# A hybrid decoder block on one core: the third part of w_ada summed on VectorE, its gates made later, and expert loads whose order turns over three experts

## What is computed

```
mod = silu(c) @ w_ada + b_ada          # 6 x 1024: shift, scale, gate for mixer and MoE
h = RMSNorm(x) * (1 + scale1) + shift1
proj = h @ w_in                        # conv B, C, u | q, k, v | gate_a, gate_b
y_a = (B * dwconv3(C * u)) @ w_out_conv ; y_b = diff_attention(q, k, v) @ w_o_attn
x = x + gate1 * ((sigmoid(ga) * y_a + sigmoid(gb) * y_b) @ w_merge)
h = RMSNorm(x) * (1 + scale2) + shift2
x = x + gate2 * MoE(h)                 # top 4 of 32 experts, clamped SwiGLU
out = RMSNorm(x)
```

## Time and profile before

| | us |
|---|---|
| median of 3 runs | 1215.8 |
| lowest, highest run | 1212.63, 1217.0 |
| the profiled execution | 1212.78 |
| its span, first to last instruction | 1211.0 |
| PE busy | 1148.4 (95%) |
| DVE busy | 409.5 (34%) |
| ACT busy | 208.7 (17%) |

### The profile page before, as it was taken

The page is one execution under the profiler, slowest core; times in us unless marked ns, Lnnn a source line. Parts: engine busy times, 40 slices in busy tenths (PEclk is TensorE's granted clock), DMA queues, the critical chain, the costliest instruction groups (busy, mean ns, idle before and its releaser), DMA issues.

```text
span 1211.0 us, 15215 instructions
## 1 busy us (share of the span) xinstructions
PE 1148.4 (95%) x6027; PEld 534.1 (44%) x6027; DVE 409.5 (34%) x795; ACT 208.7 (17%) x333; POOL 19.7 (2%) x40
## 2 busy tenths in 40 slices
PE   5999999999999999999999998989999999999997
PEld 4787899985333333333333332323333333333332
DVE  4447746663232222222222222222232222222222
ACT  4346543341011010101010101010110101010001
POOL 1000010000000000000000000000000000000000
PEclk9999999999999999999999999999999999999999
DMA  9997565798999999999999999999999999999994
GB/s 338 395 386 280 182 230 167 255 398 369 397 428 430 427 430 426 431 426 429 428 429 428 429 428 429 427 382 421 426 432 425 431 426 431 426 430 427 430 426 206
DMA packets 59394, 470.55 MB, mean 389 GB/s; under 512 B 5871, under 2 KB 11196, under 8 KB 32742
## 3 DMA queue, kind: packets, MB, share of 16 engines
q1 hardware_dynamic: 56644, 467.99, 93.5%
q10 hardware_dynamic: 2722, 2.16, 0.6%
HBM read 469.08 MB, written 1.06 MB: 388 GB/s over the span
## 4 chain that ended last, share of the span: by engine, by line
PE 65%; DMA 29%; DVE 2%; ACT 1%; SPq 1%; issue 1%; DVEq 0%; POOLq 0%; POOL 0%; ACTq 0%
PE ps L1014 19%; DMA expert<-in_w_down 16%; PE ps L783 15%; PE ps L1052 15%; DMA expert<-in_w_gate_up 12%; PE ps L988 4%; PE ps L959 2%; PE ps L727 1%; PE ps L658 1%; PE ps L940 1%; PE ps L1039 1%; ACT r_work L1254 1%; SPq L440 1%; DVE r_v L1691 1%; DMA ada_first<-in_w_ada 1%
## 5 line engine op out<-in xcount | busy, mean ns | idle before, releaser
L1014 PE MATMUL ps<-expert,r_work 128*64 128x512 f32 x2048 | 451.7, 594 | 12.3 <-DMA expert<-in_w_gate_up 11.3
L1014 PEld LDWEIGHTS ps<-expert,r_work 128*64 128x64 f32 x2048 | 146.5, 137 | 300.1 <-issue 280.1
L1052 PE MATMUL ps<-expert,r_work 128*64 128x512 f32 x1024 | 233.4, 606 | 24.1 <-DMA expert<-in_w_down 15.9
L1682 DVE TENSOR_SCALAR r_v<-ps 128x512 f32<-128x512 f32 x32 | 22.1, 692 | 371.3 <-PE ps L1014 371.3
L1052 PEld LDWEIGHTS ps<-expert,r_work 128*64 128x64 f32 x1024 | 72.8, 139 | 162.7 <-issue 136.9
L1250 ACT ACTIVATE r_v<-r_v 128x512 f32<-128x512 f32 x32 | 20.2, 630 | 713.8 <-DVE r_v L1682 713.8
L1702 DVE TENSOR_TENSOR r_work<-ps,r_gb 64x512 f32<-64x512 f32 x64 | 44.1, 689 | 169.5 <-PE ps L1052 169.0
L1364 DVE TENSOR_TENSOR w_lo<-stage,w_hi 128x2048 fp32r<-128x2048 f32 x36 | 82.2, 2289 | 55.9 <-ACT w_hi L1110 55.9
L783 PE MATMUL ps<-x_hi,w_hi 128*128 128x256 f32 x304 | 87.6, 288 | 0.0
L783 PE MATMUL ps<-x_lo,w_hi 128*128 128x256 f32 x304 | 86.0, 283 | 0.0
L783 PE MATMUL ps<-x_hi,w_lo 128*128 128x256 f32 x304 | 86.0, 283 | 0.0
(11 more groups left out here) (219 smaller groups left out, 862.3 us busy)
## 6 DMA issues: line engine op xcount, KB each, us to landing
expert<-in_w_gate_up SPq DMA_DIRECT2D x128, 2048.0 KB, 26.9
expert<-in_w_down SPq DMA_DIRECT2D x64, 2048.0 KB, 20.4
stage<-in_w_in SPq DMA_DIRECT2D x24, 1024.0 KB, 5.6
stage<-in_w_ada SPq DMA_DIRECT2D x16, 1024.0 KB, 7.7
ada_first<-in_w_ada SPq DMA_DIRECT2D x16, 256.0 KB, 6.4
ada_first<-in_w_ada SPq DMA_DIRECT2D x8, 512.0 KB, 12.2
stage<-in_w_o_attn SPq DMA_DIRECT2D x4, 1024.0 KB, 7.7
stage<-in_w_merge SPq DMA_DIRECT2D x4, 1024.0 KB, 5.8
```

The costliest lines, as they stand in the source:

```text
L1014: mm = pe.matmul(ps[CAP * g:CAP * g + CAP, j, :], xg[:, 2 * (k % 4) + k // 4, :], buf[:, col:col + 512], start=False, stop=(k == KD - 1))
L1052: mm = pe.matmul(ps[CAP * half:CAP * half + CAP, 3, :], aT[:, ch, CAP * g:CAP * g + CAP], expert[n][:, col:col + 512], start=(q == 0), sto ...
L1682: v.tensor_scalar(glu.rearrange("p (b n) -> p b n", b=2), gu[:, :, :, 0], LIMIT, None, ALU.min).then_inc(glu_ready, 1)
```

## The change

Three edits that belong together, and one of the expert loads.

- Part three of w_ada no longer goes to PE chunk by chunk. DVE scales each 128 x 2048 chunk with silu(c) per partition and adds it up in one tile, ada_acc (`ada_add`, semaphore `ada_added`). When all eight are in, PE adds the partitions with a matrix of ones: four matmuls, `ada_sum`, at the start of step 22. SP now waits for `ada_added` before it reuses a buffer that held such a chunk.
- STREAM is in another order. Part three's first four chunks are loaded behind chunks 3 to 6, part two behind 7 to 14, part three's last four behind 19 to 22. DVE adds a chunk in the step before the one it is loaded with, behind its w_lo of that step: steps 2 to 5 and 18 to 21.
- mod_step moves from steps 19, 20, 21, 22 to 20, 23, 24, 25, the late loads to 22, router weights to 24, router bias to 26. b_parts lies in the place of the keys, and ACT waits there for the scores rather than for the gates. The load of slot 2 waits for the gates too. The subtraction for lambda moves one step on.
- The order of the expert loads turns over experts 16 to 19: in front of `rest_of_next` come four, three, two and one of the slots of the expert after next.

```diff
+ADA_AT = {7 + k: ("ada", 1, k) for k in range(KD)}
+ADA_AT.update({3 + k if k < 4 else 15 + k: ("ada", 2, k) for k in range(KD)})
+ADA_SUMMED = 22
...
-         19: [("modt", 0)], 20: [("modt", 1)], 21: [("modt", 2)], 22: [("modt", 3)]}
+         20: [("modt", 0)], 23: [("modt", 1)], 24: [("modt", 2)], 25: [("modt", 3)]}
...
+            if what[0] == "ada" and what[1] == 2:
+                eng.wait_ge(ada_added, what[2] + 1)
...
-            first_of_second(2 * CATCH_UP, 0)
-            rest_of_next(2 * CATCH_UP, 0)
-            rest_of_next(2 * CATCH_UP + 1, 1)
-            first_of_second(2 * CATCH_UP + 1, 1)
+            for n in range(TWICE):
+                i, ahead = 2 * CATCH_UP + n, TWICE - n
+                some_of_second(i, n % 2, 0, ahead)
+                rest_of_next(i, n % 2)
+                some_of_second(i, n % 2, ahead, TWICE)
...
+            def ada_sum():
+
+                pe.wait_ge(mod_ready, 4)
+                pe.wait_ge(ada_added, KD)
+                for g in range(4):
+                    m = pe.matmul(ps[32 * g:32 * g + 32, 6, :], ones[:, 0:32], ada_acc[:, 512 * g:512 * g + 512],
+                                  start=True, stop=True)
+                m.then_inc(ada_used, 1)
...
+            def ada_add(k):
+
+                wait_chunk(v, ("ada", 2, k))
+                src = front_chunk(STREAM.index(("ada", 2, k)))[0][:, :]
+                if k == 0:
+                    ins = v.tensor_scalar(ada_acc, src, cs32[:, k, 0:1], None, ALU.mult)
+                else:
+                    v.wait_ge(ada_added, k)
+                    ins = v.scalar_tensor_tensor(out=ada_acc, in0=src, scalar=cs32[:, k, 0:1], in1=ada_acc,
+                                                 op0=ALU.mult, op1=ALU.add)
+                ins.then_inc(ada_added, 1)
...
+                if n + 1 in ADA_AT and ADA_AT[n + 1][1] == 2:
+                    ada_add(ADA_AT[n + 1][2])
```

More of the change, by code:

```diff
@@ L81 @@
 LAST_CHUNK = {p: CHUNK_NO[(p, 0 if p in (OC0, OC1) else 1)] for p in range(19)}
[L86 to L89, removed]
+ADA_AT = {7 + k: ("ada", 1, k) for k in range(KD)}
+ADA_AT.update({3 + k if k < 4 else 15 + k: ("ada", 2, k) for k in range(KD)})
+ADA_SUMMED = 22
+STREAM = []
+for _n in range(len(CHUNKS)):
     STREAM.append(("w", _n))
-    if _ada:
-        STREAM.append(_ada.pop(0))
+    if _n in ADA_AT:
+        STREAM.append(ADA_AT[_n])
 STAGE, WIDE, WIDE_UNTIL = 3, 5, 16
@@ L210, in block_kernel @@
         o_lo = at("o_lo", o_ol, 2048, F32R)[:, :].rearrange("p (k n) -> p k n", k=KD)
-        b_parts = at("b_parts", o_bp, 2048, F32R)
+        b_parts = at("b_parts", o_k, 2048, F32R)
         b_hi = b_parts[:, 0:1024].rearrange("p (k n) -> p k n", k=KC)
@@ L249, in block_kernel @@
         csig = r_conv[:, 1552:1560]
+        ada_acc = r_gb[:, :]
         nfb = r_gb[:, 0:D]
@@ L389, in wait_front_used @@
         def wait_front_used(eng, what):
-            if what[0] == "ada":
+            if what[0] == "ada" and what[1] == 2:
+                eng.wait_ge(ada_added, what[2] + 1)
+            elif what[0] == "ada":
                 eng.wait_ge(ada_used, KD * what[1] + what[2] + 1)
@@ L516, in _ @@
                     wait_evacuated(sp, OC1, 1)
+                    sp.wait_ge(gates_ready, 2)
                 if early is not None:
@@ L547, in first_of_second, with some_of_second @@
             def first_of_second(i, parity):
-                for j in range(TWICE):
+                some_of_second(i, parity, 0, TWICE)
+            def some_of_second(i, parity, first, end):
+                for j in range(first, end):
                     sp.wait_ge(up_used, UP_SLOTS * i + (j + 1))
@@ L558, in _ @@
                     rest_of_next(2 * m + p, p)
-            first_of_second(2 * CATCH_UP, 0)
-            rest_of_next(2 * CATCH_UP, 0)
-            rest_of_next(2 * CATCH_UP + 1, 1)
-            first_of_second(2 * CATCH_UP + 1, 1)
-            with sp.Fori(CATCH_UP + 1, final) as m:
+            for n in range(TWICE):
[3 more added lines that the diff above has]
+                some_of_second(i, n % 2, ahead, TWICE)
+            with sp.Fori(CATCH_UP + TWICE // 2, final) as m:
                 for p in range(2):
@@ L878, in _ @@
             for n in range(len(CHUNKS)):
-                what = STREAM.index(("w", n)) + 1
-                if what < len(STREAM) and STREAM[what][0] == "ada":
-                    ada_chunk(*STREAM[what][1:])
+                if n in ADA_AT and ADA_AT[n][1] == 1:
+                    ada_chunk(*ADA_AT[n][1:])
+                if n == ADA_SUMMED:
+                    ada_sum()
                 if n == 2:
@@ L1198, in _ @@
                     act.wait_ge(conv_ready, 1)
-                    act.wait_ge(gates_ready, 2)
+                    act.wait_ge(scores_done, H)
                     act.activation(b_hi, bT, ACT.Copy).then_inc(conv_hi, 1)
                 if n == LATE_LOADS:
-                    act.wait_ge(ada_used, 3 * KD)
+                    act.wait_ge(ada_added, KD)
                     for r in range(4):
@@ L1298, in _ @@
                               ps[:, 2 + b, :].rearrange("p (k n) -> p k n", k=2)).then_inc(xT_dve, 1)
[L1300 to L1303, removed]
             def bias_and_lam():
+                v.wait_ge(lam_exp, 2)
+                own.done(v.tensor_tensor(lam_s[:, 4:5], lam_s[:, 3:4], lam_s[:, 2:3], ALU.subtract))
+                own.wait()
+                v.tensor_scalar(lam_s[:, 4:5], lam_s[:, 4:5], -LAM_INIT, None, ALU.add).then_inc(lam_out, 1)
                 v.wait_ge(g_made, 1)
@@ L1513, in split_next @@
                         split(n + 2)
-                what = STREAM.index(("w", n))
-                if STREAM[what + 1:what + 2] and STREAM[what + 1][0] == "ada" and STREAM[what + 1][2] == KD - 1:
-                    mod_rows(STREAM[what + 1][1] + 2)
+                if ADA_AT.get(n) == ("ada", 1, KD - 1):
+                    mod_rows(3)
+                if n == ADA_SUMMED:
+                    mod_rows(4)
                 ends = n == LAST_CHUNK[p]
```

7 lines of the change are left out of this document (4 added, 3 removed).

## The result

| | before | after |
|---|---|---|
| median, us | 1216.3 (4 runs) | 1230.53 (4 runs, 1229.1 to 1232.67) |
| ratio to before | 1 | 1.0123, 95% interval 1.0104 to 1.0142 |
| span of the profiled execution, us | 1211.0 | 1229.6 |
| PE busy, us | 1148.4 | 1146.6 |
| DVE busy, us | 409.5 | 427.1 |

The changed kernel is slower by 1.2%, 14 to 15 us. DVE does 17.6 us more, PE 1.8 us less.

What follows compares the result with a forecast made beforehand. PE bounds the front and DMA the expert loop, and a late front arrives at the end. 1212.8 - 6.3 + 1.0 + 24.15 + 1.7 - 3.0 = 1230.4, taken as 1231 us, range 1221 to 1240.

Steps and rivals of the forecast that it cites:

- steps 3 to 6 get shorter: Front: ada chunks leave PE, but chunk 6 still lands at 61 us and product 6 starts at 65.2; -2.3 us.
- steps 15 to 18 get shorter: Front: PE is busy throughout, so these steps give all of their ada chunks' time; -4.0 us.
- wait ahead of product 21: Front: chunk 21 is issued behind an addition, lands late, and PE waits for its w_lo; +4.05 us.
- wait at ada_sum: Front: ada_sum stands ahead of product 22 and needs all eight additions, so PE waits; +20.1 us.
- ada_sum and its clock: Front, on PE: ada_sum's four matmuls cost like one ada chunk; +1.0 us, with no clock loss in this term.
- the turn: Expert loop, 795 to 805 us: the new load order removes DMA's hole and all of it counts; -3.0 us.
- the tie between front and loop: From 290 us: full slots keep DMA from working ahead, so a us lost or won before is one at the end.
- The third rival: Expert loop: the front's delay is made good, loads filling part of the 20 us; 1212 to 1222 us, 5%.
- The ring: Steps 18 to 21: split, w_lo, addition, issue and landing form a closed circle of 11.8 us against 5.75 per product.
- The clock: Front: after a long wait PE runs at the lower clock for a while, charged once; +1.7 us.
- The second rival: Front: loads are not late and only ada_sum's own wait of 7.0 us is paid; 1211.5 us, 6%.

Runs made afterwards that it cites:

- the first half alone: Kernel before, old expert load order, only part three's chunks k = 0 to 3 added on DVE, PE multiplying k = 4 to 7: 1213.62 us, ratio 0.9986.
- the two best versions: Changed kernel with ada_sum in step 23 and late additions ahead of w_lo (1206.19 us, 0.9931), or a step earlier with taps moved (1206.88 us, 0.9933).

## Why the prediction was right, point by point

The forecast was 1231 us and the median is 1230.5. That they agree to half a us is luck. The sum adds 17.6 us to the profiled execution of the kernel before, 1212.8 us. That execution was a fast one: it is 3 us under the median, and faster than each of the 40 executions of the later sessions (1212.86 us and more). Against repeated runs the change costs 15 us by the ratio. The sum was 2.6 us too high for that, and the low base hid it. The mechanism is not luck, as the terms show, from anchor to anchor in the two profiles, which differ by 18.6 us:

| term | forecast, us | measured, us | where |
|---|---|---|---|
| steps 3 to 6 get shorter | -2.3 | -3.5 | start of product 3 to start of product 7: 46.95 to 74.45 before, 48.68 to 73.57 after, with 0.9 ahead of product 3 |
| steps 15 to 18 get shorter | -4.0 | -3.6 | start of product 7 to end of product 18; a wait of 0.8 for attention is in it |
| clock in the first 30 us | none | +2.6 | 0.73 in 20 to 30 us |
| wait ahead of product 21 | +4.05 | +4.4 | |
| product 21 partly at half clock | none | +1.7 | 7.4 us rather than 5.75 |
| wait at ada_sum | +20.1 | +18.1 | |
| ada_sum and its clock | +1.0 | +1.9 | |
| products behind it partly at half clock | +1.7 | +1.6 | 13.12 rather than 11.5 us for two |
| front together | +20.6 | +22.6 | expert 0 at 312.61 rather than 290.00; the rows above add up to 23.2, and 0.6 is not accounted for |
| the turn | -3.0 | -4.0 | span +18.6 where expert 0 is +22.6 |

**What bounds the kernel.** Right, and the tie between front and loop is shown. In ten changed kernels the start of expert 0 lay between 286.72 and 312.61 us. The span followed: with the new turn it is 2.9 to 4.1 us less than the start's shift would make it, with the old one 1.6 us more (22.9 for 21.25; the first half alone, 3.5 for 1.9, and why 1.6 more there is open, since its hole at the turn is as wide as before). Nothing of a late front was made good by the loop, and of an early one (1.1, 2.8 and 3.3 us) most arrives too: against the 4.0 us of the turn, the spans of these three are 0.4 to 1.1 us short. The third rival falls.

**The ring.** Right in place, order and size. With T = 169.54 in the trace of after, the forecast had chunk 21 issued at T + 6.5, ada_sum at T + 41.9. They came at T + 6.58 and T + 41.91. Landings took 5.33, 5.09 and 5.15 us, forecast 5.3. An addition takes 2.35 us, 0.06 more than the w_lo from which it was priced. That the ring and not the amount of DVE's work is the cause is shown by the run with the additions ahead of w_lo: same work, 17.5 us less wait. The Trainium skill (DMA: Bandwidth & Descriptors, "Anatomy of one DMA — SWDGE (gpsimd) path") gives a formula for transfers of another path, from which 4.4 us for 1 MB is an estimate. The trace sides with the row of before, as the prediction did: with 4.4 us for each of the three landings ada_sum would have started 2.4 us sooner than it did.

**The clock.** The step was right that PE would run at half clock for a while after its wait, but it was charged once, and it comes after both waits. The granted clock in the stretches around them, after:

```profile
180.00:185.00 5.00, 1.49 (x13) 1.30 (x11) 1.59 (x1) 1.91 (x1) 0.00 (x0) 1.00 0.61 252
185.00:190.00 5.00, 4.15 (x22) 4.18 (x23) 4.55 (x6) 0.00 (x0) 0.00 (x0) 0.66 0.17 27
190.00:195.00 5.00, 3.32 (x28) 3.11 (x26) 0.00 (x0) 1.90 (x2) 0.00 (x0) 1.00 0.98 393
195.00:200.00 5.00, 0.00 (x0) 0.00 (x0) 4.96 (x5) 0.98 (x3) 0.00 (x0) 0.61 0.00 0
...
205.00:210.00 5.00, 0.00 (x0) 0.00 (x0) 3.25 (x2) 1.71 (x1) 0.00 (x0) 0.50 0.35 129
210.00:215.00 5.00, 3.55 (x16) 1.92 (x17) 1.99 (x2) 0.00 (x0) 0.00 (x0) 0.50 0.51 150
215.00:220.00 5.00, 5.00 (x38) 5.00 (x38) 0.00 (x0) 0.00 (x0) 0.00 (x0) 0.85 0.73 273
```

The first fall is free: it makes product 21 end 1.7 us later and so shortens the wait behind it, whose end DVE sets. That, and 0.35 us more in the first wait, is why the wait at ada_sum is 18.1 and not 20.1 us. The second one counts: 0.95 us in ada_sum and 1.6 in the two products.

**Steps 3 to 6.** The profile of after has -3.5 us where the sum had -2.3, but this does not make the step wrong. It said that chunk 6 lands at 61 us whatever the additions do, and that product 6 therefore starts at 65.2. In the profile of after PE came late by itself, because its clock had fallen: product 3 started at 48.68 rather than 46.95. Chunk 6, issued at 56.45, landed 5.7 us later, and products 4, 5 and 6 ran end to end (17.21 us in the chain). The form with the earlier additions and the later sum has the same edits in these steps, and its clock did not fall. ACT's split of chunk 6 there, and the chain around product 6:

```profile
60.73 1.92 ACT L1131 ACTIVATE w_hi<-stage 128x2048 fp32r<-128x2048 f32 x1 [1.77 <-DMA stage<-in_w_in]
63.80 1.28 issue
65.08 5.99 PE ps L803 x48
```

The load was issued at 53.42 and took 7.3 us, in a stretch of 391 GB/s. The split starts at 60.73 and product 6 at 65.08, against 61 and 65.2 in the prediction, and from product 3 to product 7 the steps give 2.0 us by the anchors of the table. So the queue was priced about right, and what the sum lacked is the clock. It did not cost its full 2.6 us either: product 7 starts 0.9 us earlier than before in the profile of after and 2.4 us earlier in this one, so 1.5 us of the fall were left by then. Four of the nine profiles with the changed start have a wait of 0.7 to 1.3 us ahead of product 6, five have none; the one of 1.3 us is that of this form. In the other three of the four (the additions ahead of w_lo, and the two with the first half alone) the wait is of another kind. The load takes 5.0 to 5.2 us but is issued at 59 us, because the first addition took 2.97 or 2.98 us rather than 1.28. In these three it started 0.3 to 0.8 us behind POOL's one long instruction there (L614 and L609, 2.2 to 2.7 us), and it ended 1.1 us behind its end; in the six others it started ahead of it. No run tested this by itself. In repeated runs the first half alone gives 1.7 us after paying 1.0 for the sum, 2.7 in all, with an interval of about 1 us on either side.

**The turn.** Right in mechanism, 1 us too small in the profiles. The prediction took the hole of 795 to 805 us alone; 805 to 810 us at 400 GB/s and 830 to 835 us at 377 GB/s are low before and not after, and are worth 0.3 and 0.6 us by the same reckoning. And the hole has no fixed width: it was 5.8 us in the changed kernel with the old turn, with a clock fall in it.

**The second rival** (only the sum's own wait, 7 us) is refuted in the changed kernel by ACT's three waits for DMA. The run with the additions ahead of w_lo comes near its number, 5.0 us, but not by its mechanism: there too ACT stands idle for 5.0 us until chunk 22 lands. With that load in time the sum's own wait was never seen alone.

**Still open.** Whether a changed start of the kernel makes the clock fall between 20 and 30 us more often; three profiles of the old front and nine of the new don't tell. And what a fourth stage buffer in steps 17 to 25 would do to the ring was not tried.

## What to carry to other kernels

Taking work off the busiest engine can cost more than it gives if the engine that gets it also holds a buffer that the next load needs (here 7.1 us off PE, and 22.5 us of waits put on it): write out the ring (landing, each reader in program order, issue) and compare it with the period it has to keep. The place of an instruction in its engine's program can matter far more than its length: 2.35 us moved ahead of 2.3 us, in each of four steps, gave back 18.8. And where one resource is saturated in a loop, look for the places where its order of requests turns, because the hole there (3.0 and 5.8 us) cost its full width here; the two best versions (0.9931 and 0.9933) have half of their gain from the new turn alone. And check the execution from which a forecast takes its base against repeated runs: one that is 3 us fast can hide an error of the sum, as it did here.

## What the runs showed of the hardware

- After a wait of 4.4 us the granted clock was at 1.2 GHz, its lower level, for a part of what followed (mean 0.66 over 185 to 190 us), and in the wait of 18.1 us it fell while PE was idle (0.50 from 200 to 215 us). The two falls made PE's work behind them 1.7 and 2.6 us longer; the first cost the kernel nothing, since DVE set when PE could go on.
- 1 MB loads on SP's queue took 5.1 to 5.3 us when issued into an empty queue (three in the ring), 5.7 us when issued 3.4 us behind another (chunk 6 of after), 6.73 us when 2.26 us behind another, at 347 GB/s, and 7.3 us in a stretch of 391 GB/s.
- scalar_tensor_tensor on two float32 tiles of 128 x 2048 took 2.34 to 2.36 us on DVE, tensor_tensor 2.29, and the first addition, a tensor_scalar with one input, 1.28 in six profiles. In three it took 2.97 or 2.98 us, and these are the three in which it started while an instruction of POOL on 128 x 2048 float32 ran.
- Two kernels with the same front on PE, and the same waits of 1.3 and 1.2 us just before, had a granted clock of 1.00 and of 0.83 in the same ten microseconds.
- After a wait of PE of 2.24 us for w_down the clock was 1.00 in one kernel, after one of 2.25 us 0.50 in another.
